# Weight-streaming matmuls whose moving rows are read, and whose outputs are written, from the last column to the first

## The reference

```
h = rms_norm(x, norm_mix[l]);  proj = h @ w_in[l]                 # 2048 -> 5120
a = sliding-window attention with sinks(q, k, v)                   # 16 query heads, 4 key heads
o = HGRN2 mixer(hq, hf, hi, hg);  yc = short convolution(cc * ch)
x = x + concat([a, o, cb * yc]) @ w_out[l]                         # 2048 -> 2048
h = rms_norm(x, norm_ffn[l]);  gate, up = split(h @ w_gate_up[l])  # 2048 -> 2 x 5632
x = x + (silu(gate) * up) @ w_down[l]                              # 5632 -> 2048
```

## Time and profile before

| What | Value |
|---|---|
| median of 3 runs (lowest to highest) | 2530.27 us (2528.61 to 2536.81) |
| the profiled execution: its own time | 2543.36 us |
| the profiled execution: span from first to last instruction | 2541.8 us |
| TensorE: matmul busy, instructions | 2525.5 us (99%), 19426 |
| TensorE: weight loads busy | 2497.6 us (98%) |
| VectorE, ScalarE, GpSimd busy | 1478.6, 1016.7, 330.0 us |
| mean granted TensorE clock | 0.998 of full speed |
| HBM | 166 GB/s over the span |

### The profile page before, as it was taken

How to read it: one execution, slowest core, us unless ns; L and a number is a source line. 1 busy time by engine, 2 the same in 40 slices (tenths; PEclk the granted TensorE clock), 3 DMA queues, 4 the chain that set the end, 5 groups by cost and what they waited for, 6 DMA issues and landing times.

```text
span 2541.8 us, 51052 instructions
## 1 busy us (share of the span) xinstructions
PE 2525.5 (99%) x19426; PEld 2497.6 (98%) x19426; DVE 1478.6 (58%) x2011; ACT 1016.7 (40%) x1412; POOL 330.0 (13%) x279
## 2 busy tenths in 40 slices
PE   9999999999999999999999999999999999999998
PEld 9999999999999999999999999999999999999998
DVE  6678787555554445555545787775555443555544
ACT  5454554333333333333334545443333333333333
POOL 2001003111110011111100200131111000111111
PEclk9999999999999999999999999999999999999999
DMA  6555445444555444444455554454444455544443
GB/s 233 168 160 182 157 146 173 157 165 165 165 171 168 157 166 165 165 165 166 165 166 166 177 174 153 142 166 166 165 165 165 166 172 158 165 165 165 167 165 136
DMA packets 116516, 420.84 MB, mean 166 GB/s; under 512 B 13840, under 2 KB 15120, under 8 KB 116368
## 3 DMA queue, kind: packets, MB, share of 16 engines
q1 hardware_dynamic: 109296, 397.72, 47.3%
q0 software_dynamic: 4112, 14.78, 1.8%
q10 hardware_dynamic: 3024, 7.16, 0.9%
HBM read 411.06 MB, written 11.87 MB: 166 GB/s over the span
## 4 chain that ended last, share of the span: by engine, by line
PE 97%; DVE 2%; ACT 1%; DMA 0%; issue 0%; DVEq 0%; SPq 0%
PE gp L1623 31%; PE gp L1625 31%; PE gp L1627 31%; PE mb L1676 1%; PE mb L1787 0%; PE mb L1800 0%; PE mb L1808 0%; DVE xl L1276 0%; DMA raw<-wstream 0%; PE mb L1685 0%; DVE wsp L789 0%; PE mb L1734 0%; ACT sc L586 0%; PE mb L1751 0%; ACT sc L584 0%
## 5 line engine op out<-in xcount | busy, mean ns | idle before, releaser
L789 DVE TENSOR_TENSOR wsp<-raw,wsp 128x1024 fp32r<-128x1024 f32 x754 | 987.8, 1344 | 360.6 <-ACT wsp L449 357.3
L449 ACT ACTIVATE wsp<-raw 128x1024 fp32r<-128x1024 f32 x754 | 769.3, 1052 | 583.2 <-PE gp L1627 548.6
L1623 PE MATMUL gp<-xh,wsp 128*128 128x288 f32 x4096 | 890.2, 299 | 2.8 <-DVE xl L1276 1.8
L1625 PE MATMUL gp<-xh,wsp 128*128 128x288 f32 x4096 | 873.5, 294 | 0.0
L1627 PE MATMUL gp<-xl,wsp 128*128 128x288 f32 x4096 | 873.1, 295 | 0.0
L1625 PEld LDWEIGHTS gp<-xh,wsp 128*128 128x128 f32 x4096 | 665.8, 189 | 0.0
L1623 PEld LDWEIGHTS gp<-xh,wsp 128*128 128x128 f32 x4096 | 653.6, 188 | 10.8 <-issue 7.1
L1627 PEld LDWEIGHTS gp<-xl,wsp 128*128 128x128 f32 x4096 | 653.7, 188 | 0.0
L1623 PE MATMUL gp<-fh,wsp 128*128 128x288 f32 x1408 | 303.8, 296 | 0.0
L1625 PE MATMUL gp<-fh,wsp 128*128 128x288 f32 x1408 | 301.0, 295 | 0.0
L1627 PE MATMUL gp<-fl,wsp 128*128 128x288 f32 x1408 | 300.6, 295 | 0.0
(11 more groups left out here) (266 smaller groups left out, 1651.6 us busy)
## 6 DMA issues: line engine op xcount, KB each, us to landing
raw<-wstream SPq DMA_DIRECT2D x754, 512.0 KB, 4.2
s<-s_cache POOLq DMA_DIRECT2D x8, 512.0 KB, 10.7
hs_out<-s ACTq DMA_DIRECT2D x8, 512.0 KB, 3.3
caches_out<-caches POOLq DMA_DIRECT2D x8, 496.0 KB, 8.8
x<-x_in ACTq DMA_DIRECT2D x4, 576.0 KB, 8.7
kct<-kt_cache POOLq DMA_DIRECT2D x4, 512.0 KB, 5.0
vct<-v_cache POOLq DMA_DIRECT2D x4, 512.0 KB, 6.5
y_out<-x SPq DMA_DIRECT2D x3, 576.0 KB, 2.9
```

Of the source, the lines that this page charges most:

```text
L449: a.activation(slab(0, slot), raw_slab(slot), ACT.Copy).then_inc(hi_ready, 1)
L789: v.tensor_tensor(slab(1, slot), raw_slab(slot), slab(0, slot).bitcast(F32), ALU.subtract).then_inc(lo_ready, 1)
L1623: t.matmul(outs[c], weights(0, slot, k, c), mv_hi, start=first, stop=False)
L1625: t.matmul(outs[c], weights(1, slot, k, c), mv_hi, start=False, stop=False)
```

## The change

In `block`, the views of the two moving rows and of the two outputs are replaced by views of the same 288 elements in descending order: the start is column 287 and the step is -1. As inputs and outputs are both turned round, column t of the result still lands at column t. The stationary pieces, their placement by parity, the number and order of the instructions, all waits and all other engines' work stay as they were.

```diff
@@ -294,6 +294,10 @@
 
             at_ = k % 2 * ODD_AT + part_at(part, slot) + k // 2 * SLAB_N + c * P
             return wsp[:, at_:at_ + P]
+
+        def backwards(row):
+
+            return bass.AP(row.tensor, row.offset + TOK - 1, [row.ap[0], (-1, TOK)])
 
         def lev_q(i):
 
@@ -1617,8 +1621,8 @@
 
             def block(slot, k, sides, bank, mv, first, end):
 
-                mv_hi, mv_lo = mv
-                outs = [gp[2 * bank + c][:, 0:TOK] for c in range(2)]
+                mv_hi, mv_lo = (backwards(v_) for v_ in mv)
+                outs = [backwards(gp[2 * bank + c][:, 0:TOK]) for c in range(2)]
                 for c in sides:
                     t.matmul(outs[c], weights(0, slot, k, c), mv_hi, start=first, stop=False)
                 for c in sides:
```

## The result

| | before | after |
|---|---|---|
| median, us (runs) | 2536.76 (6) | 2547.47 (6) |
| lowest to highest, us | 2528.61 to 2543.29 | 2545.93 to 2547.68 |
| profiled execution: own time, span, us | 2543.36, 2541.8 | 2545.93, 2544.4 |

The ratio is 1.0046, with a 95% interval of 1.0026 to 1.0065: slower by 10.7 us between the medians. The spread is as telling as the medians. Before covers 15 us, after 1.8 us. The profiled execution of before happens to be one of its slowest, so the two traces stand only 2.6 us apart in span, and have to be compared with that in mind.

The account below looks back on a forecast made before the run. The prediction took TensorE's matmul pace, 132.8 ns in `block`, to bound the kernel. It summed 2530.3 us, +20.8 us for reading rows downwards and 0 for writing outputs downwards to 2551 us, range 2480 to 2602 us.

Parts of the forecast that it names:

- What bounds the kernel: Whole kernel: TensorE, busy 99% of the span; time is a count of matmuls times the distance between starts.
- item 3: Engines and queues waiting behind TensorE: waits grow at no cost if matmuls slow; splitting still hides if they quicken.
- The distance of 132.8 ns: Block matmuls: one start to the next takes 132.8 ns, the same in both layers; 18048 of them take 2397 us.
- The 146 us for the rest: Outside the block's matmuls: the mixers' small matmuls, start and tail take 146 us, untouched by the change.
- the sum's 121.3 ns: Each block matmul: estimated time to move 288 fp32r columns, if exactly twice as fast as plain fp32's 242.5 ns.
- Item 1: Moving rows read downwards in block's 18048 matmuls: a loss of 1.15 ns each, +20.8 us; bounds -208 to +208 us.
- the extra over moving: Each block matmul: 11.5 ns beyond moving columns, 208 us in all, from fixed handover or the two reads' mutual cost.
- My reason for the sign: Moving and weight reads: climbing together from a common start is given up, so a loss, +1.15 ns per matmul.
- Item 2: Outputs written downwards in block: zero cost taken; +1980 us if steps other than +1 lose fp32r's faster movement.
- The rival of half speed: Every block matmul: columns pair only upwards, so the pace is near 242.5 ns and time 4510 us; chance 0.15.
- Nothing happens: Block matmuls: the 11.5 ns are fixed handover or go by unchanged 128-byte halves; 2530 us; chance 0.23.
- The reads get out of each other's way: Block matmuls: opposite reads meet less often; a third of 11.5 ns gone gives 2461 us, limit 2322 us; chance 0.24.

Follow-up runs that it names:

- the row stands still: Kernel before with the moving views at step 0, so all 288 columns read column 0 of the row, outputs forwards: median 2399.4 us, ratio 0.9443.
- the first set: The first four of twelve experiments, sharing a chip and the runs of the kernel before, whose median beside them was 2535.7 us.
- the weights in the other half: Split weights 128 bytes further on, in the half of a 256-byte line opposite their row's: kernel before 2546.37 us, changed kernel 2545.44 us.
- mixed halves: Placement by parity taken back, so every second row's piece starts in the opposite half: kernel before 2546.88 us, changed kernel 2552.4 us.
- The quarter line: Kernel before, forwards, with the weights 64 bytes further on, a quarter of a 256-byte line: median 2541.03 us, ratio 1.0000.

## Why the prediction was right, and where it wasn't

*What bounds the kernel*: right. In every run the time followed the pace of TensorE's block, and item 3 (what waits behind) held even at 2399 us, where matmuls took 124.4 ns: 97% of the chain that ended last was still TensorE.

*The distance of 132.8 ns*: half right. All the stretches of the earlier trace rows were of one kind, and I concluded that the pace is the same in all stages. The stretch at 1290 us in the same trace has 131.7 ns. A table over all stages would have shown it, and with it that the kernel before moves by 7 us from run to run for a reason of its own. The 146 us for the rest were too small for the same reason, since 2397 us took 132.8 ns everywhere. One more reading was loose: the trace has two rows for each plain fp32 matmul of the program (L1663 in the earlier trace rows is two calls, and x4 in the trace), so the 111 and 242.5 ns of the earlier trace rows are of a row, and the sum's 121.3 ns rests on a row being twice the time of an fp32r matmul's columns, which no run shows.

*Item 1, the reads*: the direction was right, and the runs with only the rows and only the outputs turned show that the loss comes from there. The place was also right as far as it is shown: it is the extra over moving, of which 8.4 ns vanish when the row stands still. The size was not: I took +1.15 ns, +20.8 us. The medians differ by 10.7 us, 0.59 ns per matmul. And the form of the loss was another. I expected a pace of 133.9 ns. After has 132.8, which before has as well; what is lost is the chance of 131.7. By my own last sentence, that the prediction is wrong if the pace stays and the time moves, this term failed for the FFNs of the two traces. The loss adds up so: 4.2 us over the same work in the two traces, whose FFNs have one pace, are the mixers'; and of the FFN stretches of before some half ran at the higher pace, if the groups are read by the theory (9 x 2 + 19 of 35 x 2 = 37 of 70, in the runs of the first set), one of two on average, 6.5 to 7 us. Together 10.7 to 11.2 us, against 10.7 measured. That the time came out so near the 2551 us was luck: the base of 2530.27 us, a median of three, was 6.5 us below the median of six, and the loss that I added was 10.1 us too large.

My reason for the sign, that two reads which climb together part company when one is turned, was no more than an assumption, and that the sign came out right was luck as well. No row shows in which direction the weights are read, and with the weights in the other half the same turn of the row changed nothing (2546.37 us forwards, 2545.44 us backwards, on two chips). The argument that nothing changes at the level of 128-byte halves was true as geometry, but turning the rows alone took the higher pace away, so something besides the order of the halves counts. Whether it is a finer step or a coarser one (the row also passes its lines in the other order) no run separates. The run with mixed halves shows that neighbouring rows count together, and so does the pattern of the higher pace, which repeats every second row.

*Item 2, the writes*: right to take zero. With only the outputs turned the ratio is 1.0006 (0.9988 to 1.0024). The rival of half speed is refuted for reads and writes: no pace comes near 242.5 ns. Of the two wordings in the Trainium skill, the one in "Advanced Engine Details and Errata", section "Memory Cachelines", that every two consecutive elements should be contiguous, agrees with these runs for a step of -1 (the same section also has the wide wording, which the prediction left out); "any non-contiguous AP slows matmuls significantly", in "PSUM — Partial Sum Buffer", section "Specifications (TRN2)", does not hold if a step of -1 is counted as non-contiguous.

*The other rivals.* "Nothing happens" fell with the interval, which begins at 1.0026. It was right about the FFN stretches of the two traces, though. "The reads get out of each other's way" fell for this change; the row that stands still shows that most of its 208 us can go (8.4 of 11.5 ns), but neither reversal made here collects them.

What stays open: why there are two paces and not a range of them, what at an entry decides between them, why the higher one is lost with the direction, whether the walk of the moving read costs something without the weights' load beside it, and in which direction weights are loaded. A run with the weights themselves turned round wasn't made.

## What to carry to other kernels

Before a difference of half a per cent is explained, look at the list of times of the kernel before: groups with gaps between them mean a choice that falls anew in each run, and a median then measures how often it falls which way. Take the pace of a stream in every stage, not in four stretches of one kind. Where fp32r matmuls stream with weight loads between them, the place of the weights relative to the moving row within 256 bytes is worth some 0.4% here, and so is the order of reading: of the four combinations one alone had the higher pace, and changing both did not bring it back.

## What the runs showed of the hardware

**A stream of matmuls can lock into one of two paces.** With rows read forwards and equal halves it is 131.7 or 132.8 ns per matmul, kept for 840 us of an FFN through hundreds of slabs, and it changed only where other matmuls or a pause came in between. The lower repeats with every row k, the higher with every second one. The quarter line had 132.3 ns, and the other placements and directions 132.8 to 133.1 ns in the stretches read.

**The moving read pays for where it goes.** The Trainium skill, "TensorE: Matmul & The Clock Gate", section "What happens when you issue a matmul", says that loading the next weights doesn't take SBUF read bandwidth from the running matmul. These runs show that the two reads are not quite independent for fp32r: shifting the weights alone by 128 bytes took the 131.7 ns pace away, 1.1 ns per matmul. Letting the row stand still saved 8.4 of 132.8 ns; how much of that has to do with the weights is not shown. The same page of the Trainium skill, section "Back-to-back issue gap", has a formula for an isolated matmul, which gives an estimate of 288 / 2.4 + 2.5 = 122.5 ns; the standing row comes within 2 ns of it, the walking one stays 10 ns above.

**The accumulator can be written downwards for nothing** that could be measured, from an odd last column: with only the outputs turned the stretch at 1290 us kept its 610 matmuls in 80 us, and the ratio was 1.0006 (0.9988 to 1.0024).
